# Three places of one kernel changed together: the score and projection order of the last attention layer, the order in the first layer, the convolution's output product

## What is computed

```python
def conv_mixer(h, w_in, b_glu, dw_w, dw_b, ln_g, ln_b, memq_g, w_out, mem_k, mem_v):
    ...
    c = jax.nn.silu(layer_norm(c, ln_g, ln_b))
    m = memory_attention(q_mem, memq_g, mem_k, mem_v)
    return jnp.concatenate([c, m], axis=-1) @ w_out
def swa_mixer(h, w_in, q_g, k_g, sinks, memq_g, w_out, mem_k, mem_v):
    ...
    q = rms_norm_3(proj[..., :o1].reshape(b, s, SWA_KV_HEADS, SWA_GROUP, HEAD_DIM), q_g)
    k = rms_norm_3(proj[..., o1:o2].reshape(b, s, SWA_KV_HEADS, HEAD_DIM), k_g)
    v = proj[..., o2:o3].reshape(b, s, SWA_KV_HEADS, HEAD_DIM)
    ...
    sc = jnp.einsum('bnqhgd,bnchd->bnhgqc', qb, kk).astype(jnp.float32) * (HEAD_DIM ** -0.5)
    ...
    p = jax.nn.softmax(jnp.concatenate([sc, sink], axis=-1), axis=-1)[..., :-1]
    o = jnp.einsum('bnhgqc,bnchd->bnqhgd', p.astype(vv.dtype), vv).reshape(b, s, SWA_Q_WIDTH)
    m = memory_attention(q_mem, memq_g, mem_k, mem_v)
    return jnp.concatenate([o, m], axis=-1) @ w_out
```

## Time and profile before

| | |
|---|---|
| three runs | 2086.59, 2091.14, 2091.20 us; median 2091.14 us |
| profiled execution | 2093.04 us, its span in the trace 2091.0 us |
| PE busy | 2031.1 us (97%), 10292 records |
| DVE, ACT, POOL busy | 1566.3 (75%), 1237.9 (59%), 42.0 us (2%) |
| granted TensorE clock, mean | 0.99 |
| HBM | 262 GB/s over the span |

### The profile page before, as it was taken

One profiled execution on the slowest core, in us unless ns is written; L12 is line 12 of the kernel. 1 busy time (PEld: TensorE's weight loads), 2 busy tenths in 40 slices (PEclk: granted clock), 3 DMA queues, 4 the chain that ended last, 5 costly groups with the idle time before them and its releaser, 6 DMA issues.

```text
span 2091.0 us, 29920 instructions
## 1 busy us (share of the span) xinstructions
PE 2031.1 (97%) x10292; PEld 1678.5 (80%) x10292; DVE 1566.3 (75%) x2142; ACT 1237.9 (59%) x1606; POOL 42.0 (2%) x52
## 2 busy tenths in 40 slices
PE   8999989999999999999988999999999999999998
PEld 7786879769997769998756888888888888888887
DVE  6456776785664855554257989999898989999898
ACT  2211456544434454443256878788888878888886
POOL 0000000000000000001000000000000000000000
PEclk9999999999999999999989999999999999999999
DMA  9777743355552315554316999999999999999996
GB/s 323 173 273 272 267 165 132 101 181 189 180 194 82 101 60 202 188 186 120 121 42 244 392 363 401 387 359 393 356 392 356 404 372 381 393 358 391 356 398 245
DMA packets 275462, 548.72 MB, mean 262 GB/s; under 512 B 29484, under 2 KB 81205, under 8 KB 275125
## 3 DMA queue, kind: packets, MB, share of 16 engines
q1 hardware_dynamic: 266189, 528.46, 68.7%
q0 software_dynamic: 3984, 14.68, 2.3%
q10 hardware_dynamic: 5208, 4.49, 1.2%
HBM read 537.11 MB, written 10.48 MB: 262 GB/s over the span
## 4 chain that ended last, share of the span: by engine, by line
PE 90%; DVE 7%; ACT 1%; SPq 1%; issue 1%; DMA 0%; DVEq 0%; ACTq 0%
PE sum L1578 12%; PE bank L1560 10%; PE bank L1562 10%; PE bank L1561 10%; PE bank L738 9%; PE sum L1202 7%; PE bank L1219 4%; PE bank L1221 3%; PE bank L1220 3%; PE sum L800 3%; PE bank L754 1%; PE sum L1309 1%; PE bank L1546 1%; PE sum L780 1%; PE sum L1592 1%; PE sum L781 1%
## 5 line engine op out<-in xcount | busy, mean ns | idle before, releaser
L3015 DVE TENSOR_TENSOR x_lo<-ring,x_hi 128x1024 fp32r<-128x1024 f32 x672 | 781.0, 1221 | 44.8 <-ACT x_hi L2132 24.4
L2132 ACT ACTIVATE x_hi<-ring 128x1024 fp32r<-128x1024 f32 x648 | 667.1, 1058 | 119.7 <-PE bank L1562 65.5
L1560 PE MATMUL bank<-x_hi,hg_hi 128*128 128x512 f32 x896 | 354.9, 396 | 1.6 <-DVE xtr L2972 1.6
L1562 PE MATMUL bank<-x_hi,hg_lo 128*128 128x512 f32 x896 | 350.1, 391 | 0.0
L1561 PE MATMUL bank<-x_lo,hg_hi 128*128 128x512 f32 x896 | 349.5, 390 | 0.0
L2340 DVE TENSOR_TENSOR w_lo<-ring,w_hi 128x1024 fp32r<-128x1024 f32 x130 | 158.1, 1225 | 114.6 <-ACT w_hi L1942 112.8
L738 PE MATMUL bank<-hT,ring 128*128 128x256 f32 x1024 | 231.2, 387 | 3.6 <-DMA ring<-in_w_in 1.8
L738 PEld LDWEIGHTS bank<-hT,ring 128*128 128x128 f32 x1024 | 198.3, 195 | 35.5 <-issue 7.8
L1942 ACT ACTIVATE w_hi<-ring 128x1024 fp32r<-128x1024 f32 x130 | 136.6, 1058 | 148.1 <-PE bank L1221 76.7
L1562 PEld LDWEIGHTS bank<-x_hi,hg_lo 128*128 128x128 f32 x896 | 168.5, 188 | 35.9
L1560 PEld LDWEIGHTS bank<-x_hi,hg_hi 128*128 128x128 f32 x896 | 168.7, 188 | 34.9 <-DVE xtr L2972 1.7
(11 more groups left out here) (527 smaller groups left out, 2819.7 us busy)
## 6 DMA issues: line engine op xcount, KB each, us to landing
ring<-in_sw_we_gate SPq DMA_DIRECT2D x114, 1024.0 KB, 7.2
ring<-in_sw_we_up SPq DMA_DIRECT2D x112, 1024.0 KB, 7.4
ring<-in_sw_we_down SPq DMA_DIRECT2D x112, 1024.0 KB, 7.3
ring<-in_w_in SPq DMA_DIRECT2D x36, 1024.0 KB, 7.7
ring<-in_w_ff SPq DMA_DIRECT2D x32, 1024.0 KB, 5.3
ring<-in_ada_w SPq DMA_DIRECT2D x24, 1024.0 KB, 9.1
ring<-in_w_out SPq DMA_DIRECT2D x12, 1024.0 KB, 7.0
ring<-in_cv_w_gate SPq DMA_DIRECT2D x11, 1024.0 KB, 5.1
```

The lines of the kernel that those rows point to most:

```text
L1560: mm(ps[b][:, :], hg_hi[:, k, :], hi[:, cols], start=(k == 0), stop=False)
L1562: last = mm(ps[b][:, :], hg_lo[:, k, :], hi[:, cols], start=False, stop=(k == KC - 1))
L2132: go(f(x_hi[:, hp % MSLOTS, :], ring[:, s, lo:lo + PIECE // 2], ACT.Copy), c.sig("hi_ready", hp))
L3015: v.tensor_tensor(x_lo[:, hp % MSLOTS, :], ring[:, s, lo:lo + PIECE // 2], x_hi[:, hp % MSLOTS, :].bitcast(F32), ALU.subtract).then_inc(c. ...
```

## The change

The last attention layer does the scores of the first two pairs ahead of the value product. Keys of each key head are written into rows of their own, 128 partitions with 64 of them zero (`swk_rows`, `memk_rows`), so that each score matmul reads all 128 partitions of the queries; POOL fills and copies these rows. In the first layer `ada(1)` moves ahead of `ada_sum(2)`, piece 2 and the splits of piece 3 move back by a step, with other places for the high parts, and ACT's wait ahead of the second layer's splits is for an earlier piece. The convolution's output pieces 0, 1 and 2 are done in three fp32r passes, with the high and low parts made by ACT and DVE. The computed function is the same.

```diff
-B1_OUT = {1: 4, 3: 5, 4: 6, 5: 7, 6: 0, 8: 1, 9: 2, 11: 3}
+B1_OUT = {1: 4, 3: 5, 4: 6, 5: 7, 6: 0, 8: 1, 10: 2, 11: 3}
 B1_ORDER_OUT = list(B1_OUT.values())
-B1_SPLIT = {0: 4, 2: 5, 3: 6, 4: 7, 5: 0, 6: 1, 7: 2, 8: 3}
+B1_SPLIT = {0: 4, 2: 5, 3: 6, 4: 7, 5: 0, 6: 1, 7: 2, 9: 3}
...
-        rows_hi[B1_ORDER_OUT[-1]] = (rows_hi_last[:, 0, :], rows_hi_last[:, 1, :])
+        rows_hi[B1_ORDER_OUT[-2]] = (rows_hi_last[:, 0, :], junk_r[:, :])
+        rows_hi[B1_ORDER_OUT[-1]] = (rows_hi_last[:, 1, :], rows_hi_odd[:, :])
...
+        over_h = dT_hi[:, :, :].rearrange("p (a b) n -> p a (b n)", a=2)
+        over_p = probT_r[:, :, :].rearrange("p a b -> p (a b)")
+        cv_hi = {0: (d_hi[:, 0, :], d_hi[:, 1, :]), 1: (d_hi[:, 2, :], over_p), 2: (over_h[:, 0, :], over_h[:, 1, :])}
+        mix3_hi = [dT_lo[:, k, :] for k in range(CC)]
+        mix3_lo = [dT_lo[:, 6 + k, :] for k in range(2)] + [mix3_low[:, k, :] for k in range(4)]
...
+        swk_rows = [U(2, 2, S, off=512), U(4, 2, S, off=512)]
+        memk_rows = [U(1, 2, S, off=512), U(3, 2, S, off=512)]
...
-            sum_rows("cv", "cv_out", 4, mix3, lambda k: pe.wait_ge(*c.at("conv_act", 2 * k + 1)), (0, 1, 2), 3, 2)
+            for k in range(3):
+                lo = ring_r[:, W.place(("cv_out", k)), :].rearrange("p (k n) -> p k n", k=2)
+                for t in range(NT):
+                    for h in range(2):
+                        for j in range(2):
+                            if t + h == 0:
+                                pe.wait_ge(*c.at("cv_low", k, j))
+                                pe.wait_ge(*c.at("conv_split", 2 * k + j))
+                            m_hi, m_lo = (x[2 * k + j][:, t * P:(t + 1) * P] for x in (mix3_hi, mix3_lo))
+                            hi, cs = cv_hi[k][j], slice(h * 512, (h + 1) * 512)
+                            mm(acc[2 * t + h][:, :], m_hi, hi[:, cs], start=False, stop=False)
+                            mm(acc[2 * t + h][:, :], m_hi, lo[:, j, cs], start=False, stop=False)
+                            last = mm(acc[2 * t + h][:, :], m_lo, hi[:, cs], start=False, stop=(k == 2 and j == 1))
+                        if k == 2 and t + h < 2:
+                            last.then_inc(c.sig("sums", "cv", 2 * t + h).sem, 1)
+                s = c.sig("piece_used", "cv", k)
+                last.then_inc(s.sem, 1)
+                free([("cv_out", k)], s)
...
-            b = J.fill(pe, "swv")
-            for t in range(NT):
-                for k in range(KC):
-                    last = mm(ps[b][:, t * 256:(t + 1) * 256], hT[:, k, t * P:(t + 1) * P], w[k][:, 0:256],
-                              start=(k == 0), stop=(k == KC - 1))
-            free(keys, done(last, "swv"))
-            rms_spread(1, 2)
...
+                    pe.wait_ge(*c.at("memory_rows"))
...
-                            g, y, x = h // 6, 64 * (h % 6 // 3), h % 3
-                            last = mm(ps[b][:, col:col + nk * P], swq[y:y + 64, 3 * g + x, t * P:(t + 1) * P],
-                                      swk[y:y + 64, g, 0:nk * P], start=True, stop=True)
+                            g, y, x = h // 6, h % 6 // 3, h % 3
+                            last = mm(ps[b][:, col:col + nk * P], swq[:, 3 * g + x, t * P:(t + 1) * P],
+                                      swk_rows[g][:, y, 0:nk * P], start=True, stop=True)
...
-                            y, x = 64 * (h % 2), i - SW_PAIRS
-                            last = mm(ps[b][:, col:col + nk * P], mqT[y:y + 64, x, t * P:(t + 1) * P], memkT[y:y + 64, x, :],
+                            y, x = h % 2, i - SW_PAIRS
+                            last = mm(ps[b][:, col:col + nk * P], mqT[:, x, t * P:(t + 1) * P], memk_rows[x][:, y, :],
...
-            pe.wait_ge(*J.emptied("swv"))
-            for i in range(SW_PAIRS + SM_PAIRS + 3):
+            pair_scores(0)
+            pair_scores(1)
+            b = J.fill(pe, "swv")
+            for t in range(NT):
+                for k in range(KC):
+                    last = mm(ps[b][:, t * 256:(t + 1) * 256], hT[:, k, t * P:(t + 1) * P], w[k][:, 0:256],
+                              start=(k == 0), stop=(k == KC - 1))
+            free(keys, done(last, "swv"))
+            rms_spread(1, 2)
+            for i in range(2, SW_PAIRS + SM_PAIRS + 3):
                 if i < SW_PAIRS + SM_PAIRS:
                     pair_scores(i)
-                if i == 1:
+                if i == 2:
                     rms_spread(2, 1)
                 if 2 <= i < SW_PAIRS + SM_PAIRS + 2:
                     pair_turn(i - 2)
                 if i in SW_BETWEEN:
                     sw_out(SW_BETWEEN[i])
+                if i == 3:
+                    pe.wait_ge(*J.emptied("swv"))
...
-                if n == len(B1_ORDER_OUT) - 1:
-                    act.wait_ge(*J.full("b1S", HEADS1 - 1))
+                if n == len(B1_ORDER_OUT) - 2:
+                    act.wait_ge(*J.full("b1S", HEADS1 // 2 - 1))
+                    act.wait_ge(*J.full("ada", ADA[11]))
                 elif n >= 2:
+                    if n == len(B1_ORDER_OUT) - 1:
+                        act.wait_ge(*J.full("b1S", HEADS1 - 1))
...
-            act.wait_ge(*c.at("piece_used", "b1", B1_ORDER_OUT[-2]))
+            act.wait_ge(*c.at("piece_used", "b1", B1_ORDER_OUT[-3]))
...
+            def cv_high(k):
+                act.wait_ge(*W.ready(("cv_out", k)))
+                for j in range(2):
+                    go(f(cv_hi[k][j], ring[:, W.place(("cv_out", k)), j * D:(j + 1) * D], ACT.Copy), c.sig("cv_high", k, j))
             taps(DIAGS, len(CONV_TAPS))
+            cv_high(0)
+            cv_high(1)
             for k in range(CC):
                 act.wait_ge(*c.at("centred", k))
                 do(f(sq3[:, k, :], cT[:, k, :], ACT.Square), c.sig("cvar_in", k))
+            cv_high(2)
...
-            copy(flat(swv), ("swv",))
...
+                if i == 1:
+                    copy(flat(swv), ("swv",))
...
+            ada(1)
             ada_sum(2)
-            ada(1)
...
+            def cv_low(k):
+                for j in range(2):
+                    dve.wait_ge(*c.at("cv_high", k, j))
+                    x, cs = W.place(("cv_out", k)), slice(j * D, (j + 1) * D)
+                    v.tensor_tensor(ring_r[:, x, cs], ring[:, x, cs], cv_hi[k][j].bitcast(F32), ALU.subtract)\
+                        .then_inc(c.sig("cv_low", k, j).sem, 1)
+            cv_low(0)
+            cv_low(1)
             for k in CONV_PE:
                 dve.wait_ge(*c.at("tap_used", (k - 3) * CONVW - 1))
                 do(v.tensor_scalar(cT[:, k, :], acc[k - 4][:, 0:S], vec("cv_dw_b_3", k), None, ALU.add), c.sig("cmean_in", k))
             do(v.tensor_scalar(lnw[:, 0, :], bank("cmean")[:, 0:S], 1.0 / CONV, None, ALU.mult), J.free("cmean"))
             for k in range(CC):
                 v.tensor_tensor(cT[:, k, :], cT[:, k, :], lnw[:, 0, :], ALU.subtract).then_inc(c.sig("centred", k).sem, 1)
+            cv_low(2)
             dve.wait_ge(*J.emptied("cvar"))
             do(v.reciprocal(lnw[:, 1, :], lnw[:, 1, :]))
             for k in range(CC):
                 v.tensor_tensor(cT[:, k, :], cT[:, k, :], lnw[:, 1, :], ALU.mult).then_inc(c.sig("conv_normed", k).sem, 1)
+            for k in range(CC):
+                dve.wait_ge(*c.at("conv_act", k))
+                split(mix3_hi[k], mix3_lo[k], mix3[:, k, :], c.sig("conv_split", k))
...
-            for g in range(2):
-                rms_invert(g)
+            def group_ready(g):
                 rms_apply(g, 0, (flat(swq[:, 3 * g:3 * g + 2, :]), 0, 512))
-                rms_apply(g, 1, (swq[:, 3 * g + 2, :], 0, S), (swk[:, g, :], S, S))
+                b = bank("swb", g, 1)
+                do(v.tensor_tensor(swq[:, 3 * g + 2, :], swq[:, 3 * g + 2, :], b[:, 0:S], ALU.mult))
+                if g == 0:
+                    dve.wait_ge(*c.at("rows_cleared"))
+                for y in range(2):
+                    rows = slice(H64 * y, H64 * (y + 1))
+                    do(v.tensor_tensor(swk_rows[g][rows, y, :], swk[rows, g, :], b[rows, S:2 * S], ALU.mult), J.free("swb", g, 1) if y else None)
                 do(v.tensor_copy(xtr[:, 6, g:g + 1], ones[:, 0:1]), c.sig("sw_ready", g))
+            rms_invert(0)
+            group_ready(0)
+            rms_invert(1)
             rms_invert(2)
...
+                if i == 1:
+                    group_ready(1)
...
+            for x in (*swk_rows, *memk_rows):
+                do(g.memset(x, 0.0), c.sig("rows_cleared") if x is swk_rows[1] else None)
+            for x in range(2):
+                for y in range(2):
+                    rows = slice(H64 * y, H64 * (y + 1))
+                    do(g.tensor_copy(memk_rows[x][rows, y, :], memkT[rows, x, :]), c.sig("memory_rows") if x + y == 2 else None)
```

5 lines of the change are left out of this document (3 added, 2 removed).

## The result

| | before | after |
|---|---|---|
| median of five runs each, side by side | 2089.94 us (2086.58 to 2091.20) | 2075.55 us (2075.36 to 2078.19) |
| profiled execution, its span | 2093.04, 2091.0 us | 2075.36, 2073.5 us |
| granted TensorE clock, mean | 0.99 | 0.995 |

The account below looks back on a forecast made before the run. PE's own work was taken as the bound (busy 2031 of 2091 us). Savings of 2.4 + 3.6 + 3.7 + 3.5 = 13.2 us took the profiled 2093.04 to 2079.8, as a median 2077.9 us; range 2072.0 to 2084.0.

Parts of the forecast that it names:

- Conditioning sum: First layer: PE's 2.39 us wait for the bank DVE takes late goes away; -2.4 us, bounds 0 and 2.4.
- Nothing late in its place: First layer, conditioning sum: DVE's eight instructions end some 1.2 us later, but the sum reading them comes a projection later.
- Last two pieces: First layer's output product: piece 2 runs without its 2.72 us stop, norm starts earlier; -3.6 us, bounds 2.7 and 4.1.
- Convolution: Convolution output: 72 passes in 17.8 us replace 48 fp32 records in 22.53, starting 1.0 late; -3.7 us, bounds 2.0 and 5.1.
- Attention: Last attention layer: early scores let divisions and the first output sum come earlier; -3.5 us, bounds 0 and 7.
- The walk along VectorE: Last attention layer: DVE (VectorE) sets the pace after norming group 1; first output sum 3.7 to 4.4 us earlier.
- Less 0.65 for the first memory pair: Last attention layer: padded, its 8 records take 1.79 us instead of 1.14, taken off the gain.
- price little of it: Last attention layer: padded scores partly keep the clock up, little counted since DVE and the banks set the pace.
- Its own signs: Observations listed beforehand as showing the forecast right or wrong: waits, stops, pass times, score lengths, low clock across the values.
- The first: Attention padding costs more than it gives, losing 4.3 us, 3.6 more than counted; 2081.5 us, chance 0.10.
- The second: Clock stays up in convolution product and attention: 1.4 us more there, 2 to 3 here; 2073.9 us, chance 0.15.
- The third and fourth: A first-layer or convolution wait returns, 2081.5 to 2084, chance 0.10; clock stays low from attention's values wait, 2094.5, chance 0.03.

## Why the prediction was right

- **Conditioning sum**, forecast 2.4: 2.55, and 2.7 when undone. "Nothing late in its place" held: B did not grow. How much of the larger loss in the total, when undone, is the wait's doing stays open.
- **Last two pieces**, forecast 3.6: 3.7, 3.5 when undone; every start within 0.3 us.
- **Convolution**, forecast 3.7: 3.35. The start came 0.65 late instead of 1.0, since ACT's root ran earlier, and the 72 passes took 18.4 us instead of 17.8, as passes are 0.232 apart rather than 0.228 (16.7) and the low stretch cost 1.6, not 1.4. The 0.232 stood in the prediction's own paragraph on the first layer. The splits stayed under cover, as said. The argument for the low stretch, that a longer wait brings it again, is only half borne out: of the eight profiles with passes and a wait of 2.8 us, six had a stretch or two in C, of the four with a shorter wait one.
- **Attention**, forecast 3.5: 4.26. The walk along VectorE was right to 0.3 us (its idle time, the norming, the divisions, the first sum). The sum failed at two terms. "Less 0.65 for the first memory pair": the pair took 0.85 longer, but the wait behind it fell by 0.70, and it cost 0.15 at most. Without this term the forecast had been 4.15. And "price little of it", of the clock: the padding by itself gives 1.8 us. For the order by itself that leaves 2.5: the walk assumed that PE keeps up with VectorE, and it is the padding that lets PE do so. The sum for this place came near, but the forecast put down to the order what the two edits do together.
- **The rest**: 13.9 us of the change against 13.2; that two parts missed in opposite directions, by 0.35 and 0.76, helped. The profile's 3.15 us in the middle are chance of the stretches, and more than the "2 us either way" of the forecast; the medians, 14.4 us apart, show little of them.
- **Its own signs.** Two signs of being wrong came: four heads' scores took 2.89 us, over 2.66, and VectorE waited 2.14 us for `cv_high`. Neither cost anything, since both lay ahead of a wait for something later. The 2.66 was a spacing of starts and was compared with the length of a merged row, which has the end of its last record in it. The passes took 18.4 us, outside "16.4 to 17.8". The first output sum of the attention layer came 17.3 us earlier in the profile, 13.7 without the 3.15 and 0.5 that are not the change's; about 14 were foreseen. The other signs fell as the forecast has them.
- **Rivals.** The first (padding costs more) had the sign wrong. The second (clock stays up in both places) was nearly true of the attention (one stretch instead of five) but not of the convolution, whose fall comes and goes: none in six of fourteen profiles, one of these six in fp32. The third and fourth did not happen; the clock stayed up across the values.

## What to carry to other kernels

Where an engine is bound by another's order, walk along the waited-for engine and look for idle time ahead of a step that was written too early; that walk was right to 0.3 us, and its next use gave 3.4 us more. Price longer instructions ahead of a wait at nothing until the wait is used up. To prove parts of some 3 us in 2080, compare stages of profiles cut at the same instructions and with the same count of low-clock stretches, not medians of five runs.

## What was not expected of the hardware

- Score products on 64 of 128 rows went with more low clock than padded ones in each of three pairs, also where the waits left were the same (1.10 and 1.09 us). Full rows, half of them zeros, were worth 1.5, 1.8 and 2.3 us in the stage, net of the overlap of row halves that they give up. Why narrow rows do this, no run here shows.
- The low clock comes in stretches of 3.41 us, each worth 1.6 us where PE is the bound, at the same few places (near 45, 105, 304 to 312, 650, 700 and 757 us), and in a given execution it comes or stays away. Over the 101 executions of this study, each compared with the mean of its own kernel, 0.001 less of mean clock went with 1.3 us more time, and taking that out lowers their standard deviation from 1.9 to 1.0 us.
